# Two FFN loops on TensorE: all input blocks of one PSUM bank in a row, then the next bank

## The reference

```python
def rmsnorm(x, g):
    xf = x.astype(jnp.float32)
    r = lax.rsqrt(jnp.mean(xf * xf, axis=-1, keepdims=True) + NORM_EPS)
    return (xf * r).astype(x.dtype) * g

def swiglu(x, wg, wu, wd):
    return (jax.nn.silu(x @ wg) * (x @ wu)) @ wd

h_p = h_p + swiglu(rmsnorm(h_p, norm_ffn_g[layer]), w_gate[layer], w_up[layer], w_down[layer])
h_s = h_s + swiglu(rmsnorm(h_s, norm_ffn_g[layer]), w_gate[layer], w_up[layer], w_down[layer])
```

## Time and profile before

| | |
|---|---|
| Time, median of 3 runs | 2622.5 us (2621.45 to 2626.61) |
| The profiled execution: its own time | 2624.54 us |
| Its span, first to last instruction | 2622.8 us |
| Mean granted TensorE clock | 0.99 of full speed |
| TensorE (PE) busy | 2533.9 us, 17835 matmuls |
| VectorE (DVE) busy | 1717.4 us |
| ScalarE (ACT) and GpSimd (POOL) busy | 999.9 and 999.6 us |

### The profile page before, as it was taken

How to read it: one execution, slowest core, us unless ns; L and a number is a source line. 1 busy time by engine, 2 the same in 40 slices (tenths; PEclk the granted TensorE clock), 3 DMA queues, 4 the chain that set the end, 5 groups by cost and what they waited for, 6 DMA issues and landing times.

```text
span 2622.8 us, 44346 instructions
## 1 busy us (share of the span) xinstructions
PE 2533.9 (97%) x17835; PEld 2420.2 (92%) x17835; DVE 1717.4 (65%) x1937; ACT 999.9 (38%) x1480; POOL 999.6 (38%) x616
## 2 busy tenths in 40 slices
PE   8999989999999999999999999999989999999998
PEld 7989988999999999988888888889989999999997
DVE  4244498556666756768788778895785555567565
ACT  4122153222222111267777777783432222221113
POOL 4643335888985776100000000000245565552110
PEclk9999999999999999999999999999999999999999
DMA  4111223545445665322222231244222222234211
GB/s 131 41 42 34 74 76 96 164 151 163 154 146 193 227 216 168 147 90 81 65 89 84 88 95 61 75 140 162 82 81 83 66 82 76 88 131 167 96 66 75
DMA packets 271134, 284.93 MB, mean 109 GB/s; under 512 B 14810, under 2 KB 213778, under 8 KB 270930
## 3 DMA queue, kind: packets, MB, share of 16 engines
q1 hardware_dynamic: 252770, 272.79, 31.7%
q10 hardware_dynamic: 18160, 9.31, 1.2%
HBM read 195.37 MB, written 86.67 MB: 108 GB/s over the span
## 4 chain that ended last, share of the span: by engine, by line
PE 80%; DVE 11%; issue 4%; ACT 2%; DMA 1%; SPq 0%; ACTq 0%; POOL 0%; DVEq 0%
PE ps L1318 25%; PE ps L1407 15%; PE ps L1146 10%; PE aux L1536 8%; PE aux L1318 4%; PE ps L1453 3%; PE ps L1481 3%; PE ps L1435 2%; PE ps L1801 2%; PE ps L1465 2%; PE aux L1547 1%; PE aux L1500 1%; DVE h L2925 1%; PE aux L1489 1%; DVE sp_part_odd L2985 1%
## 5 line engine op out<-in xcount | busy, mean ns | idle before, releaser
L1318 PE MATMUL ps<-s_hi,ring 128*128 128x264 f32 x2016 | 377.5, 286 | 11.0 <-DVE h L2744 7.3
L1065 POOL TENSOR_TENSOR ring<-w_raw,ring 128x512 fp32r<-128x512 f32 x44 | 61.6, 1400 | 843.7 <-ACT ring L1969 843.7
L1407 PE MATMUL ps<-s_hi 128*128 128x352 f32 x1008 | 327.5, 325 | 10.7 <-DVE h L2933 3.8
L1318 PEld LDWEIGHTS ps<-s_hi,ring 128*128 128x128 f32 x2016 | 317.4, 190 | 12.6 <-DVE h L2744 8.2
L1407 PE MATMUL ps<-s_hi,s_lo 128*128 128x352 f32 x1008 | 326.1, 324 | 0.0
L1407 PE MATMUL ps<-s_lo,s_hi 128*128 128x352 f32 x1008 | 324.5, 322 | 0.0
L1318 PE MATMUL ps<-s_lo,ring 128*128 128x264 f32 x1008 | 287.2, 285 | 0.0
L2933 DVE TENSOR_TENSOR h<-h,ps 128x1056 f32<-128x1056 f32 x144 | 180.2, 1252 | 146.8 <-PE ps L1407 145.4
L1065 POOL TENSOR_TENSOR ring<-ring_plain,ring 128x512 fp32r<-128x512 f32 x90 | 160.8, 1803 | 260.5 <-DVE w_hi_plain L2615 213.4
L1969 ACT CAST ring<-ring_plain 128x512 fp32r<-128x512 f32 x90 | 52.0, 619 | 408.6 <-DVE ring_plain L2608 402.2
L1407 PEld LDWEIGHTS ps<-s_hi 128*128 128x128 f32 x1008 | 189.5, 188 | 14.8 <-DVE h L2933 6.3
(11 more groups left out here) (386 smaller groups left out, 6826.3 us busy)
## 6 DMA issues: line engine op xcount, KB each, us to landing
hid_kept<-h SPq DMA_DIRECT2D x44, 528.0 KB, 6.2
a_plain<-hid_kept SPq DMA_DIRECT2D x44, 528.0 KB, 5.6
w_raw<-in_w_gate_dram SPq DMA_DIRECT2D x44, 512.0 KB, 5.1
w_hi<-kept_hi SPq DMA_DIRECT2D x30, 512.0 KB, 4.0
w_lo<-kept_lo SPq DMA_DIRECT2D x30, 512.0 KB, 5.3
h_kept<-h SPq DMA_DIRECT2D x24, 528.0 KB, 3.3
h<-h_kept SPq DMA_DIRECT2D x24, 528.0 KB, 6.7
w_raw<-in_w_down_dram SPq DMA_DIRECT2D x24, 512.0 KB, 4.6
```

Of the source, the lines that this page charges most:

```text
L1065: gp.tensor_tensor(lo, src, as32(hi), ALU.subtract).then_inc(part_ready, 1)
L1318: last = mm(pairs[bank][:, c, 0:QC], w[:, ks], x[:, k, c * QC:c * QC + QC], start=(fresh and k == 0 and n == 0), stop=(k == HK - 1 and n = ...
L1407: last = mm(out[:, c, 0:CH], w[:, ns], x[:, c * CH:c * CH + CH], start=(f == 0 and m == 0), stop=(f == 1 and m == 2))
```

## The change

For units from the third on (u at least 2), `product` gets loops of its own: the half c outside, the input block k inside, so that 12 matmuls go to one bank and then 12 to the other. In `down` the third c becomes the outer loop and the hidden block f the inner one: six matmuls to each bank in a row. The waits for hidden block and weight block f of a group's first tile are made for c = 0 alone, so both come within the first six matmuls. The number, shapes and operands of the matmuls and all semaphores' updates stay.

```diff
@@ -1305,6 +1305,16 @@
                     pe.wait_ge(part_ready, parted_at(layer, u, m))
                     hi, lo = ring_slot(layer, u, m)
                     x_hi, x_lo = moving_of(layer, m)
+                    if u >= 2:
+                        for c in range(2):
+                            for k in range(HK):
+                                ks = slice(k * P, k * P + P)
+                                for n, (w, x) in enumerate(((hi, x_hi), (hi, x_lo), (lo, x_hi))):
+                                    last = mm(pairs[bank][:, c, 0:QC], w[:, ks], x[:, k, c * QC:c * QC + QC],
+                                              start=(fresh and k == 0 and n == 0), stop=(k == HK - 1 and n == 2),
+                                              skip_group_check=True)
+                        last.then_inc(mult_done, 1)
+                        return
                     for k in range(HK):
                         if u < 2 and m == 1:
                             pe.wait_ge(in_ready, a_ready(layer, k))
@@ -1396,13 +1406,13 @@
                             bank_after(NU - 1, "c12")
                         out = ps[:, 3 * (n % 2):3 * (n % 2) + 3, :]
                         ns = slice(n * P, n * P + P)
-                        for f in range(2):
-                            if n == 0:
-                                pe.wait_ge(hid_ready, 2 * (FP * layer + i) + f + 1)
-                                pe.wait_ge(wd_ready, 2 * FP * layer + 2 * i + f + 1)
-                            hi, lo = wd_parts(layer, i, f)
-                            hid_hi, hid_lo = hid_parts(layer, i, f)
-                            for c in range(NC):
+                        for c in range(NC):
+                            for f in range(2):
+                                if n == 0 and c == 0:
+                                    pe.wait_ge(hid_ready, 2 * (FP * layer + i) + f + 1)
+                                    pe.wait_ge(wd_ready, 2 * FP * layer + 2 * i + f + 1)
+                                hi, lo = wd_parts(layer, i, f)
+                                hid_hi, hid_lo = hid_parts(layer, i, f)
                                 for m, (w, x) in enumerate(((hi, hid_hi), (hi, hid_lo), (lo, hid_hi))):
                                     last = mm(out[:, c, 0:CH], w[:, ns], x[:, c * CH:c * CH + CH],
                                               start=(f == 0 and m == 0), stop=(f == 1 and m == 2))
```

## The result

The changed kernel takes 2632.3 us (median of 8 runs, 2628.6 to 2636.3), the kernel before 2624.6 us in 8 runs (2621.5 to 2627.0): a ratio of 1.0029, 95% interval 1.0020 to 1.0038. That is 7.7 us slower, and 2632.3 lies above the upper end of the predicted range. The forecast stood on 2622.5 us, the median of three runs; five more runs moved it to 2624.6. So 2.1 of the 6.3 us between forecast and result are the base; the change itself was forecast at 3.5 us and came at 7.7. The profiled execution took 2634.5 us with a span of 2631.6 us; the one of before had 2622.8.

The account below looks back on a forecast made before the run. TensorE, busy 97% of the span, was taken as the bound, through matmul pace and a few short waits. Terms 0.97 + 1.46 + 1.1 = 3.5 us on the median 2622.5 gave 2626.0 us, range 2619.5 to 2630.5.

Parts of the forecast that it names:

- Turns between banks: In products and down tiles, 2184 fewer switches of matmuls from bank to bank; priced at 0, gain at most 2.4 us.
- The bound on the side of a loss: Limit on what fewer bank turns could cost: none, because the row that never turns is the fastest of three.
- Nothing is released earlier: Products and down tiles: the semaphore still goes up at the last matmul, evacuation reads all banks at once; priced 0.
- no new wait ahead of products: Gate and up products: every wait stands ahead of the first matmul, so starts and ends stay; priced at 0.
- no wait in the other 19 groups: Down groups after each layer's first: second hidden block not waited for; priced 0, at most 0.4 us.
- The moved wait: Layer 0's first down tile: six matmuls come after the wait for the second hidden block, not hidden, +0.97 us.
- Layer 1: First down group: the moved wait's 0.97 us is hidden, but a fall of the clock adds +1.1 us.
- The fall of the clock in layer 0: After the first down tile's idle of about 2.67 us, the granted clock falls to 0.50, costing +1.46 us.
- second rival: Clock stays low twice as long behind both layers' first-tile idles: 6.5 us in sum, 2629.0 us; chance 0.12.
- Catch: 0 to 0.97, taken 0.: Layer 0 near 876.70 us, where VectorE sets the pace: how much of the 0.97 us is given back, taken 0.
- a short fall that meets the VectorE-bound stretch badly: Case for a slower result: a short low-clock period followed by trouble where VectorE sets the pace; chance 0.03.
- third rival: Bank turns in products and down tiles cost 1.1 ns each, so fewer gain 2.4 us: 2623.6 us; chance 0.10.

## Why the prediction was wrong, point by point

- *Turns between banks, taken as 0.* Right about their size, not about the sign: the new order is 10.5 ns longer per product in layer 1 and 8.5 ns shorter per down tile. The bound on the side of a loss, set to none because the one-bank row was the fastest, was wrong: about 2.3 us over 280 products by the traces. Rows of two other loops gave no bound for this one.
- *Nothing is released earlier, no new wait ahead of products, no wait in the other 19 groups.* Right: the waits for low parts are still two and two.
- *The moved wait, +0.97 us in layer 0.* Right at the tile: with the idle filled, the end of tile 0 was 1.0 us later. By itself it would have cost nothing by group 3, where the same kernel had made it up.
- *Layer 1.* Forecast +1.1 us with a short fall of the clock, measured +0.85: idle 2.42 us for 2.48, clock 0.50 for 3.3 us. The closeness is partly luck: with the same first tile, other traces have +0.6 to +2.2 in these two groups.
- *The fall of the clock in layer 0.* The mechanism was right, the term was mis-sized: 1.46 us forecast, 3.5 - 1.0 = 2.5 us measured. The clock was down for 6.8 us, not for 3.4. That is the second rival's mechanism (chance 0.12), for one layer of the two.
- *"Catch: 0 to 0.97, taken 0."* This is the step that failed. It saw that VectorE sets the pace around 876 us, and that its work there starts from TensorE's tile; from this it took that lateness passes through unchanged or is partly made up. GpSimd's work in that stretch does not start from TensorE's tile. It stayed where it was while VectorE's came late, and 3.5 us of lateness became 6.7; with 3.6 us of useless work in place of the fall of the clock it became 6.8. Lateness of 1.0 us, on the other hand, was made up whole. So the catch was neither 0 nor a share of the lateness, but depended on which of GpSimd's operations the late ones met. Rows for this stood in the trace before: additions of the same shape at 1.25 and at 3.34 us.
- *The sum.* 3.5 us forecast, 7.7 measured by the medians. The 8.8 us between the two traces are 1.0 for the wait, 2.5 for the fall of the clock, 3.3 for the second group of layer 0, 0.85 for layer 1, about 2 for the products and -1 for the down tiles. With the fall of layer 0 at its measured size and all else as forecast the sum would be 4.6 us; the echo in the second group is the larger miss. The chances gave 0.15 to slower, of which 0.03 to a short fall that meets the VectorE-bound stretch badly; the case that came was a long fall with an echo behind it, which no rival held. (In the third rival, 6.2 us over 2184 turns are 2.8 ns, not 2.9.)

## What to carry to other kernels

A reordering that leaves every count alone still decides how much work stands ahead of a wait. Look for the tile in which a wait binds: reordering the 36 matmuls of two such tiles, which put six in each behind the wait, cost as much as the whole change within the intervals, and filling the idle with useless matmuls took the loss away again. The same lateness can be made up or doubled further on. When a step comes late, don't ask only what waits for it; ask which engine's work beside it keeps its own time (here transfers set it), and what the two will now meet.

## What the runs showed of the hardware that was not expected

- A granted clock of 0.50 for 6.8 us behind idles of 1.40 and 2.61 us with 0.5 us of work between them, where an idle of 2.15 us in the kernel before was followed by 3.4 us of it, and in three other traces idles of 2.08 to 2.14 us likewise, but in five more idles of 2.12 to 2.16 us by none. Behind the long pair itself one trace of five kernels had 3.4 us, the others 6.8. What the clock does behind an idle of 2 us can't be told from its length alone.
- An operation of VectorE with both inputs in SBUF took, for one shape, 1.25 us while GpSimd was idle and between 1.25 and 4.02 us beside it (3.39 in the stretch above); with one input in PSUM always 1.25.
- Twelve matmuls of 264 columns in a row to one bank of two are 10.5 ns longer per 24 in layer 1 than threes in turn; six matmuls of 352 columns in a row to one bank are 8.5 ns shorter per 18 in these two traces, 5.5 to 8.5 in the others of the new order against the usual 158.40 us of the old. The first number comes back in each trace; the cause was not looked for.
